# Where the moving operands of a two-block transformer kernel start, relative to its weights, modulo 256 bytes

## The reference

```python
def _swiglu(x, w_in, w_out):
    gate, up = jnp.split(x @ w_in, 2, axis=-1)
    return (jax.nn.silu(gate) * up) @ w_out

for i in range(DEPTH):                      # first block, one layer
    h = h + 0.5 * _swiglu(_rmsnorm(h, ffn1_norm[i]), ffn1_w_in[i], ffn1_w_out[i])
    z = _rmsnorm(h, mix_norm[i]) @ w_in[i]  # convolution and gated linear attention
    h = h + jnp.concatenate([y_conv, y_gla], axis=-1) @ w_out[i]
    h = h + 0.5 * _swiglu(_rmsnorm(h, ffn2_norm[i]), ffn2_w_in[i], ffn2_w_out[i])
    gate = jax.nn.sigmoid(_rmsnorm(h, ple_norm[i]) @ ple_w_gate[i])
    h = h + gate * (p[i] @ ple_w_proj[i])
...
for i in range(DEPTH_2):                    # second block, two layers
    h = modulate(rms_norm(x, ln_ffn1[i]), sh1, sc1)
    x = x + 0.5 * g1[:, None, :] * swiglu(h, ffn1_wg[i], ffn1_wu[i], ffn1_wd[i])
    ...                                     # attention (i = 0) or spatial gating (i = 1)
    x = x + 0.5 * g3[:, None, :] * swiglu(h, ffn2_wg[i], ffn2_wu[i], ffn2_wd[i])
    x = rms_norm(x, ln_out[i])
```

## Time and profile before

| | |
|---|---|
| median of 3 runs | 1509.78 us (1509.22 to 1510.27) |
| the profiled execution, whole | 1507.29 us |
| its span, first to last instruction | 1505.5 us |
| PE, PEld busy | 98%, 87% of the span |
| DVE, ACT, POOL busy | 78%, 54%, 3% |
| chain that ended last | PE 86%, DVE 7%, ACT 4% |
| mean granted TensorE clock | 0.998 of full |

### The profile page before, as it was taken

The page is one execution under the profiler, slowest core; times in us unless marked ns, Lnnn a source line. Parts: engine busy times, 40 slices in busy tenths (PEclk is TensorE's granted clock), DMA queues, the critical chain, the costliest instruction groups (busy, mean ns, idle before and its releaser), DMA issues.

```text
span 1505.5 us, 22326 instructions
## 1 busy us (share of the span) xinstructions
PE 1473.1 (98%) x9258; PEld 1314.9 (87%) x9258; DVE 1177.2 (78%) x1394; ACT 820.0 (54%) x998; POOL 49.6 (3%) x40
## 2 busy tenths in 40 slices
PE   7999999899999999999999899999999999999998
PEld 6888889898888998888888888889888889988887
DVE  6988889689889778889767798898866566786654
ACT  6655354575553575554577665555655445565442
POOL 1000015200000000000000000000000000000000
PEclk9999999999999999999999999999999999999999
DMA  8988955279889559889534398897655555465551
GB/s 287 310 295 287 339 194 167 84 250 313 297 284 330 178 191 303 296 289 311 168 113 142 128 304 294 288 325 253 191 188 182 184 166 169 141 221 180 186 184 68
DMA packets 275972, 341.69 MB, mean 227 GB/s; under 512 B 6931, under 2 KB 256939, under 8 KB 275872
## 3 DMA queue, kind: packets, MB, share of 16 engines
q1 hardware_dynamic: 273904, 334.74, 67.3%
q0 software_dynamic: 1968, 5.54, 1.1%
HBM read 339.18 MB, written 2.63 MB: 227 GB/s over the span
## 4 chain that ended last, share of the span: by engine, by line
PE 86%; DVE 7%; ACT 4%; issue 1%; DMA 1%; DVEq 0%; SPq 0%; ACTq 0%
PE banks L1691 43%; PE banks L1692 22%; PE banks L1623 5%; PE banks L1624 5%; PE banks L1625 5%; DVE w_lo L993 1%; ACT w_hi L536 1%; DVE xn L1064 1%; DVE ada_acc L1111 1%; ACT xs L566 1%; DVE x_res L1137 1%; PE banks L1763 1%; ACT xn L555 1%; DVE xs L1012 1%; DMA ada<-in_ada_w 0%
## 5 line engine op out<-in xcount | busy, mean ns | idle before, releaser
L1691 PE MATMUL banks<-xs,w_hi 128*128 128x512 f32 x1952 | 682.7, 393 | 3.2 <-DVE w_lo L993 3.0
L993 DVE TENSOR_TENSOR w_lo<-raw,w_hi 128x2048 fp32r<-128x2048 f32 (+1 forms) x241 | 537.9, 2237 | 161.5 <-ACT w_hi L536 161.3
L536 ACT ACTIVATE w_hi<-raw 128x2048 fp32r<-128x2048 f32 (+1 forms) x249 | 464.8, 1870 | 214.9 <-PE banks L1692 169.7
L1692 PE MATMUL banks<-xs,w_lo 128*128 128x256 f32 x1952 | 547.6, 281 | 0.0
L1691 PEld LDWEIGHTS banks<-xs,w_hi 128*128 128x128 f32 x1952 | 366.4, 188 | 88.4 <-DVE w_lo L993 4.3
L1691 PE MATMUL banks<-g_pair,w_hi 128*128 128x512 f32 x1056 | 366.9, 391 | 0.0
L1692 PEld LDWEIGHTS banks<-xs,w_lo 128*128 128x128 f32 x1952 | 366.8, 188 | 0.0
L1692 PE MATMUL banks<-g_pair,w_lo 128*128 128x256 f32 x1056 | 295.7, 280 | 0.0
L1691 PEld LDWEIGHTS banks<-g_pair,w_hi 128*128 128x128 f32 x1056 | 197.5, 187 | 43.2
L1692 PEld LDWEIGHTS banks<-g_pair,w_lo 128*128 128x128 f32 x1056 | 199.6, 189 | 0.0
L1111 DVE SCALAR_TENSOR_TENSOR ada_acc<-ada,c_act,ada_acc 128x1152 f32<-128x1152 f32 x124 | 175.2, 1413 | 12.3 <-DMA ada<-in_ada_w 9.7
(11 more groups left out here) (302 smaller groups left out, 1694.9 us busy)
## 6 DMA issues: line engine op xcount, KB each, us to landing
ada<-in_ada_w SPq DMA_DIRECT2D x128, 576.0 KB, 6.9
raw<-in_ffn_wg SPq DMA_DIRECT2D x44, 1024.0 KB, 5.5
raw<-in_ffn_wu SPq DMA_DIRECT2D x44, 1024.0 KB, 5.5
raw<-in_ffn_w_in SPq DMA_DIRECT2D x43, 1024.0 KB, 7.1
raw<-in_ffn_wd SPq DMA_DIRECT2D x32, 1024.0 KB, 5.2
raw<-in_ffn_w_out SPq DMA_DIRECT2D x16, 1024.0 KB, 6.4
raw<-in_ffn_wd SPq DMA_DIRECT2D x16, 768.0 KB, 4.9
raw<-in_attn_w_qkv SPq DMA_DIRECT2D x12, 1024.0 KB, 5.3
```

The lines of the kernel that those rows point to most:

```text
L536: act.activation(w_hi[:, s, 0:width(c)], raw[:, s, 0:width(c)], ACT.Copy).then_inc(hi_ready, 1)
L993: dve.tensor_tensor(w_lo[:, s, 0:width(c)], raw[:, s, 0:width(c)], w_hi[:, s, 0:width(c)].bitcast(F32), ALU.subtract).then_inc(lo_ready, 1)
L1691: pe.matmul(o, wh[:, k, m], pair, start=first, stop=False, skip_group_check=True)
L1692: return pe.matmul(o[:, 0:T], wl[:, k, m], pair[:, 0, :], start=False, stop=last, skip_group_check=True)
```

## The change

Rows of `xs` become 320 floats (1280 bytes) instead of 272 (1088 bytes), with 32 floats ahead of the first row and 16 behind the last, so that the tiles after `xs` start 20672 instead of 17408 bytes behind its beginning. To make room, `ada` shrinks, three of the six constant matrices and `b_mix` move into `arena`, the constants come in two DMAs instead of one (and are waited for as two), and the `FILL` matmuls have 384 columns instead of 512.

```diff
-XS_ROW = T + 16
+XS_ROW = T + 64
+XS_LEAD, XS_GAP = 32, 16
...
-        xs = sb("xs", [P, 2, KT, XS_ROW], F32R)
+        xs_flat = sb("xs", [P, XS_LEAD + 2 * KT * XS_ROW + XS_GAP], F32R)
+        xs = xs_flat[:, XS_LEAD:XS_LEAD + 2 * KT * XS_ROW].rearrange("p (a k t) -> p a k t", a=2, k=KT)
...
-        ada_flat = sb("ada", [P, 4 * D])
+        ada_flat = sb("ada", [P, 14 * T])
...
-        consts = sb("consts_sb", [P, 6, P])
-        tri, low_mask, up_mask, ident, causal, pair_ones = (consts[:, i, :] for i in range(6))
+        consts = sb("consts_sb", [P, 3, P])
+        ident, causal, pair_ones = (consts[:, i, :] for i in range(3))
...
+        masks = carve(3 * P).rearrange("p (i n) -> p i n", i=3)
+        tri, low_mask, up_mask = (masks[:, i, :] for i in range(3))
...
-        b_mix = ada_flat[0:2, 2 * D + KT * P:2 * D + 2 * KT * P]
+        top[0] = KEPT
+        b_mix = carve(KT * P, 2)
...
-            pool.dma_start(consts[:, :, :], a["consts"]).then_inc(consts_in, 16)
+            pool.dma_start(consts[:, :, :], a["consts"][:, 3:6, :]).then_inc(consts_in, 16)
+            pool.dma_start(masks, a["consts"][:, 0:3, :]).then_inc(consts_in, 16)
...
-                dve.wait_ge(consts_in, 16)
+                dve.wait_ge(consts_in, 32)
...
-                    pe.wait_ge(consts_in, 16)
+                    pe.wait_ge(consts_in, 32)
...
-                        pe.matmul(bank[MISC][:, :], ones_d[:, :], consts[:, 0:4, :], start=True, stop=True,
+                        pe.matmul(bank[MISC][:, 0:3 * P], ones_d[:, :], consts[:, :, :], start=True, stop=True,
```

## The result

The changed kernel takes 1519.47 us (median of 3 runs, 1516.67 to 1520.73) against 1509.78: a ratio of 1.0061, interval 1.0042 to 1.0081. It is slower by 0.6%, where 1496.3 was forecast, and lies 3.5 us above the range. The profiled execution took 1516.67 us, that of before 1507.29.

The account below looks back on a forecast made before the run. PE, busy for 98% of the span, was taken as the bound. Terms of -8.1 (`xs` pairs), -2.9 (`g_pair` pairs) and -2.5 (`cs` and `p`) sum to -13.5 us, giving 1496.3 us from the median 1509.78; range 1478 to 1516.

Parts of the forecast that it names:

- The rule weighed in the prediction: On weight loads beside matmuls: separate read ports, so place would cost nothing and the forecast sum would be 0.
- The side edits: Constants in two DMAs, shorter `FILL`, moved `ada` and `b_mix`: each costed at 0, constants 0.55 us without cover.
- The term for `cs` and `p`: 624 matmuls moving to distance 192: from 120 to 116 ns each, -2.5 us (bounds -4.4 to 0).
- the last four matmuls of row 3 in the earlier trace: 256-column matmuls on the `xs` row at distance 192, 112.5 ns each: read as the settled time there.
- a settled pair = 2 * (settled matmul of 256 columns) + 106.7: Relation from distance 0 (moving row minus weights, modulo 256 bytes): gave low ends 343.3 (`xs`) and 332.7 ns (`g_pair`).
- `g_pair` pairs: 1056 pairs moving from distance 0 to 192: from 346.7 to 344 ns each, -2.9 us (-14.8 to +8.8).
- The pair at 355 ns in the earlier trace: Two pairs on the `xs` row at distance 192, 0.71 us together: the high end for pairs with `g_pair`.
- `xs` pairs: 1952 pairs, every row now at distance 128: from 349.2 to 345 ns each, -8.1 us (-11.5 to +1.6).
- Other matmuls with `xs`: 2112 matmuls in `mm3`, token-major and first chunks: 118.2 ns now, 118.3 at distance 128, so 0 (-11.0 to +3.8).
- The slower one: Rival: pairs with `g_pair` stay at 355 ns, +8.8 us, those with `xs` gain nothing: 1518.6 us; chance 0.13.
- the two cases that rest on the relation: The forecast itself (1487 to 1503 us, chance 0.42) and all products settling as the relation says (1479.1 us, 0.17).
- only steadiness counts: Rival: pairs with `xs` reach the 346.7 ns of a fixed distance, nothing else moves: -4.9 us, 1504.9 us; chance 0.15.

## Why the prediction was wrong

**What held.** PE bounds the kernel, and the place modulo 256 bytes changes what a product costs: 1501.96 and 1518.59 us come from two kernels that differ in `XS_LEAD` and `XS_GAP` alone. The rule weighed in the prediction (the Trainium skill, "TensorE: Matmul & The Clock Gate", section "Step-by-step: what each phase is for": independent read ports, no read bandwidth taken from the running matmul) does not agree with that. The side edits cost nothing, as costed (ratio 1.0002). The term for `cs` and `p` had the right sign: -2.5 forecast, -2.0 measured; the last four matmuls of row 3 in the earlier trace rows had shown its end, 112.5, and 113.3 came. That the sum fits is in part luck: 116 was a middle value, and 113.3 throughout would have given 6.7 * 624 = -4.2. Of this a stretch without pauses like that from 1290 us got its share (-0.9), those with waits around 290 and 840 us only 0.4 each, and near 841 us the matmul took 117.8 at the same distance. The weights came in time; the idle time before the pairs fell to 2.5 us.

**The step that failed** is "a settled pair = 2 * (settled matmul of 256 columns) + 106.7". It was fitted at one distance. At 192 the matmul settles at 113.3 (117.8 in shorter stretches) and the relation gives 333.3 (342.3): measured 353.3. At 128 it gives at most 346.7: measured 351.1. At 32, 340.0 to 342.3: measured 346.7. At distance 0 itself the run with everything at 0 has 120.0 for the single matmul and both 346.7 and 353.3 for the pair. The exactness that I took for a mechanism was one of two outcomes at one place. The shortest matmul of 256 columns goes with one of the slowest pairs, so the one shape says nothing of the other.

**`g_pair` pairs**, -2.9 forecast, +6.9 measured, inside the bounds of -14.8 to +8.8. The middle of the two bounds was taken because "these rows show nothing of the low end". The high end was a pair, at that distance, on this engine; the low end was a relation. The pair at 355 ns in the earlier trace rows was the better witness: 353.3 came.

**`xs` pairs**, -8.1 forecast, +2.9 measured, outside the bound of +1.6 (1.9 * 1952 = +3.7 by the settled time, and 0.7 less idle time before the pairs). The step was "nearer to the relation, since now the distance no longer changes". Both halves fell: the relation as above, and steadiness by the kernel whose rows alternate between 0 and 128 (348.3 ns, less than the 351.1 of 128 alone). The high end, 350 from two pairs, was 1.1 ns too low. The two-pairs-per-row chunk of the changed kernel, PE's timeline in the place of the earlier trace rows, shows what a mean over two pairs hides:

```profile
327.72 0.40 PE L1697 MATMUL banks<-xs,w_hi 128*128 128x512 f32 x1
327.95 0.28 PE L1698 MATMUL banks<-xs,w_lo 128*128 128x256 f32 x1
328.07 0.40 PE L1697 MATMUL banks<-xs,w_hi 128*128 128x512 f32 x1
328.31 0.28 PE L1698 MATMUL banks<-xs,w_lo 128*128 128x256 f32 x1
328.43 0.39 PE L1697 MATMUL banks<-xs,w_hi 128*128 128x512 f32 x1
328.65 0.28 PE L1698 MATMUL banks<-xs,w_lo 128*128 128x256 f32 x1
328.77 0.40 PE L1697 MATMUL banks<-xs,w_hi 128*128 128x512 f32 x1
```

The first two wide matmuls are followed after 0.23 and 0.24 us, the third after 0.22. At the trace's own resolution the starts repeat after three pairs, 234/120, 233/120, 224/122 ns, 1053 in all: 351.0 a pair. Two pairs out of a period of three give 349.5, 350.0 or 353.5, by where they are cut.

**Other matmuls with `xs`**, 0 forecast, +2.8 measured, inside -11.0 to +3.8: at 128 the matmul of 256 columns settles at 120.0 in the stretches from 212 and 1278 us and at 118.7 in others, where I had 118.3 from six in a row.

**The rivals.** The slower one came true in its mechanism and in its number: pairs of `g_pair` stay near 355 ns and `xs` gains nothing, 1518.6; measured 1519.47 with 353.3 and 351.1. What the text held against it, that "at distance 0 too a first pair is slower than a settled one", took for granted that settling leads to the fast time. It got 0.13 against 0.59 for the two cases that rest on the relation. That only steadiness counts (346.7 at any fixed distance) is refuted by 350.0, 351.1 and 353.3 at 96, 128 and 192.

**What stays open:** why a distance has the lasting times that it has, what exactly picks between two of them, and whether 256 bytes is the period everywhere (`g_pair` at 32 and at 288 modulo 512 takes the same 346.7; at 0 the one run at 256 modulo 512 has the slow time in all six stretches). The runs show that it is picked at the beginning of a stretch, that the same stretch can go either way in different kernels, and that at 0 `g_pair` can take either time behind `xs` pairs of one and the same time. What one kernel does from execution to execution was profiled once for each.

## What to carry to other kernels

Where back-to-back matmuls set the time, read it from the distance between starts over hundreds of them, stretch by stretch, and price a new placement by rows of the same shape in the same order, never through another shape. When two bounds are far apart and one of them is a measured instance while the other is a formula fitted at one point, take the measured one. Where the layout leaves a choice, try it on the whole program: here placing every moving row 32 bytes beyond the weights modulo 256 gave the fast time in every stretch and 0.5%, while 128 and 192 cost 0.6%.

## What was not expected of the hardware

A stream of equal pairs does not have one rate at one placement. It falls into one of a few exactly repeating patterns, 346.7, 348.9, 350.0, 351.1, 353.3 or 360.0 ns a pair, and keeps it for hundreds of pairs; at distances 0, 16 and 64 two of them were seen in one execution of one program. At distance 16 the choice is worth 13.3 * 320 = 4.3 us in each stretch of 320 pairs.

Single executions also differ by what the granted clock does around a layer of small products. PE in windows of 4 us (from, to: us, busy and count, PEclk, DMA share, GB/s), the kernel before:

```profile
840.00:844.00 4.00, 3.40 (x28) 1.00 0.02 4
844.00:848.00 4.00, 2.44 (x20) 1.00 0.08 9
```

The run with the side edits alone:

```profile
840.00:844.00 4.00, 2.82 (x14) 0.67 0.01 4
844.00:848.00 4.00, 3.26 (x24) 0.90 0.00 0
```

PE has pauses here in both. In the second the granted clock falls to the 1.2 GHz level for a part of the two windows, which by an estimate from these rows costs up to (0.33 + 0.10) * 4 = 1.7 us, about the 1.3 us by which its span (1506.8) exceeds that of the earlier trace rows; its median equals that of the kernel before. A single execution can be off by that much, and the comparisons above that rest on one execution are read from the pairs and not from the whole time.
